# Gated linear attention: the read-out matmuls issued head by head instead of chunk by chunk

## The chip, the cores and the metric

The kernel runs on one core of a Trainium2 chip. The metric is the device time of one execution in microseconds (us); lower is better. The profile is that of one execution, recorded by the hardware profiler; its times are counted from the first instruction.

## The reference

The program computes two model blocks, each with two layers, on 512 tokens of 1024 channels (and, in the first block, 256 context tokens). The change lies in the second block, in its gated linear attention (GLA) with 4 heads, key width 64, value width 128 and chunks of 64 tokens. Each layer runs it twice: forward over time and backward over time. Per direction:

```
b = cumsum(log decay) within a chunk;  ref = b in the middle of the chunk
q_in = q * exp(b - ref);  k_in = k * exp(ref - b)
A = where(mask, q_in @ k_in^T, 0)          # 64x64 per chunk and head
o_intra = A @ v                            # inside the chunk
state_n = state_(n-1) * decay + k_state^T @ v      # 64x128 per head, chunk after chunk
o_inter = (q * exp(b)) @ state             # what earlier chunks contribute
o = o_intra + o_inter                      # forward and backward are summed, then RMS-normalised
```

## The kernel before

All activations lie channel-major in SBUF, 128 channels by up to 512 tokens. The large products split each fp32 operand into a high and a low part and run three matmuls (hi*hi, hi*lo, lo*hi); `single`, called through `in_unit(n)`, is one such product of 24 matmuls (lines 841 on). Weights stream from HBM through a ring of four slots: SyncE loads, ScalarE (line 1178) makes the high part, GpSimd (line 464) the low part. Every engine has its own program, written out by hand in order, and they meet at semaphores; nothing is reordered by a scheduler.

In a second-block layer TensorE interleaves the input products `in_unit(2)` to `in_unit(18)` with the pieces of the GLA. These are, for a direction d (0 forward, 1 backward):

- `turned_keys(d)` (line 902): 8 transposes of 128x128; ScalarE copies them.
- `updates(d, p)` (line 918): for a pair of heads, 16 matmuls of 64 rows by 64 columns that make k^T v of each chunk; VectorE runs the recurrence over chunks (lines 2448 and 2450).
- `a_tiles(d, t0)` (line 932): the scores of two 128-token tiles, 4 heads each; contraction over the 64 key channels, so each matmul uses 64 of the array's 128 rows. Heads 0 and 2 (e = 0) take rows 0 to 63, heads 1 and 3 (e = 1) rows 64 to 127. VectorE masks them (`masked`, line 2461).
- `o_tile(d, t)` (lines 945 and 955), which the change touches: the output of a 128-token tile. It waits once, for the masked scores; nothing inside it waits. Line 945 is `A @ v`: 4 matmuls, one for each head, that contract over 128 tokens and use all 128 rows, 128 columns of output. Line 955 is `q @ state`: for each of the tile's two 64-token chunks and each head one matmul that contracts over 64 key channels (64 rows, again halves by e = head % 2) and writes 64 columns. Head h accumulates in its own PSUM bank (bank 4 + h). One chunk of each direction has no earlier state and so no such matmul: chunk 0 forward (in tile 0), chunk 7 backward (in tile 3).

All of these operands are fp32. The hardware runs such a matmul as two passes, and the trace records each pass: 4 matmuls are 8 records, 8 matmuls 16.

The order on TensorE around it is: `a_tiles(0,0)`, `in_unit(8)`, `o_tile(0,0)`, `o_tile(0,1)`, `a_tiles(0,2)`, `in_unit(9)`, `o_tile(0,2)`, `o_tile(0,3)`, `turned_keys(1)`, `in_unit(10)`, five matmuls of a sum of squares (line 1011), `updates(1,0)`; and in the backward direction the same from `a_tiles(1,0)`, ending with `in_unit(16)` after `o_tile(1,3)`. VectorE's own order has, beside the GLA's element-wise work, `unit_out(n)` (line 2386), which empties the product of `in_unit(n)` out of PSUM, and, in the first of the two layers alone, the rotation tables (lines 2336 to 2354), which stand between `unit_out(9)` and `unit_out(10)`. The fourth of the five matmuls of line 1011 writes the PSUM bank that `unit_out(10)` empties.

Of the kernel before, what the change touches and what calls it, by code (L numbers as in the profile page):

```python
# [24 lines left out]
P = 128  # L25
# [23 lines left out]
GLA_HEADS, GLA_PAIRS, GLA_C = 4, 2, 64  # L49
# [81 lines left out]
def two_blocks(nc, weights, ada_w, pool_w, vec1_d, vec2_d, gla_w_d, x_d, cond_d, ple_d, pos_d, consts_d, rope_d,  # L131
# [4 lines left out]
    with ctx:  # L136
# [42 lines left out]
        PS = ctx.enter_context(nc.psum_tensor("ps", [P, SLOTS * 1024], f32))  # L179
        ADA_PS = 3 * 1024 + 512  # L180

        def ps(s, a=0, b=None):
            return PS[:, s * 1024 + a:s * 1024 + b]
# [14 lines left out]
        def ada_sums(p, q=slice(0, P)):  # L198
# [26 lines left out]
        GF, GQI, GKI, GQX, GKS, GKT, GST, GAM = (M0, M0 + 1024, M0 + 2048, M0 + 3072, M0 + 4096, M0 + 5120,  # L225
                                                 M0 + 6144, M0 + 8192)
# [76 lines left out]
        def on(l, name):  # L303

            if (l // LAYERS, name) not in named:
                named[l // LAYERS, name] = sem(f"block{l // LAYERS}_{name}")
            return named[l // LAYERS, name]

        def at_least(l, name, n):

            return on(l, name), n + per_layer[name] if l % LAYERS else n
# [19 lines left out]
        def halves(a):  # L331

            return a.rearrange("p (a b) -> p a b", a=2)
# [9 lines left out]
        def latent(buf, n):  # L343

            if n < 2:
                return buf[:, :].rearrange("p (c t) -> p c t", c=CH)[:, 4 + 2 * n:6 + 2 * n, SEQ:TOK]
            return halves(buf[:, n * TOK:n * TOK + SEQ])
# [5 lines left out]
        def slot_of(l, st, n):  # L353

            return (UNIT0[l, st] + n) % SLOTS

        def taken(l, st, t, k):

            return k + USE[l, st][t] + 1
# [115 lines left out]
        def _(pe):  # L475
# [361 lines left out]
            def block2(l):  # L837
# [38 lines left out]
                def gv(rows, t, h):  # L876
                    c = (2 * t + h // 2) * TOK + SEQ + (h % 2) * P
                    return X[rows, c:c + P]

                every = slice(0, P)  # L880
# [56 lines left out]
                def o_tile(d, t):  # L937
                    first = 0 if d == 0 else GLA_CHUNKS - 1
                    pe.wait_ge(*at_least(l, "a_read", d * 4 + t + 1))
                    if d == 0 and t == 0:  # L940
                        for s in (2, 3):
                            pe.wait_ge(tile_free[s], taken(l, "gla_o", s, 0))
                    for h in range(GLA_HEADS):
                        o0 = 2048 + h * 512
                        nc.tensor.matmul(PS[:, o0 + t * P:o0 + (t + 1) * P], gv(every, t, h),
                                         AR[:, GAM + (t % 2) * 512 + h * P:GAM + (t % 2) * 512 + (h + 1) * P],
                                         start=(d == 0 and t == 0), stop=False, skip_group_check=True)
                    todo = [n for n in (2 * t, 2 * t + 1) if n != first]
                    for n in todo:
                        for h in range(GLA_HEADS):  # L950
                            p, e = h // 2, h % 2
                            o0 = 2048 + h * 512
                            q0 = GQX + p * SEQ + n * GLA_C
                            s0 = GST + (p * GLA_CHUNKS + n) * P
                            last = nc.tensor.matmul(PS[:, o0 + n * GLA_C:o0 + (n + 1) * GLA_C],
                                                    AR[64 * e:64 * e + 64, s0:s0 + P], AR[64 * e:64 * e + 64, q0:q0 + GLA_C],
                                                    start=False, stop=(d == 1 and t == 3 and n == todo[-1]),
                                                    skip_group_check=True)
                    last.then_inc(on(l, "o_mm"), 1)
# [18 lines left out]
                for u in range(SLOTS):  # L978
                    s = slot_of(l, "gv", u)
                    pe.wait_ge(units_split, nth_done(l, "gv", u))  # L980
                    for n, (w, act) in enumerate(((WH, XH), (WH, XL), (WL, XH))):
                        for k in range(2):
                            for t in range(4):
                                c = 2 * u + k
                                last = nc.tensor.matmul(PS[:, 2048 + t * SEQ:2048 + (t + 1) * SEQ], act[:, c * TOK + t * P:c * TOK + (t + 1) * P],  # L985
                                                        w[:, s * UNIT + k * 512:s * UNIT + (k + 1) * 512],
                                                        start=(c == 0 and n == 0), stop=(c == CH - 1 and n == 2))
# [8 lines left out]
                a_tiles(0, 0)  # L996
                in_unit(8)
                o_tile(0, 0)
                o_tile(0, 1)
                a_tiles(0, 2)  # L1000
                in_unit(9)
                o_tile(0, 2)
                o_tile(0, 3)
                turned_keys(1)
                in_unit(10)
                for n in range(Q_CH + KV_CH):
                    s, first, end, k_use = (1, 0, Q_CH, 3) if n < Q_CH else (0, Q_CH, Q_CH + KV_CH, 4)
                    if n == first:
# [3 lines left out]
                                     start=n == first, stop=n == end - 1).then_inc(on(l, "rmsq_used"), 1)  # L1012
# [28 lines left out]
                for at_, j in enumerate(UQ_ITEMS):  # L1041
                    t = at_ % 2
                    pe.wait_ge(tile_free[t], taken(l, "uq", t, at_ // 2))
                    if j in ("rope0", "rope1", "rope2"):
                        n = int(j[-1])
# [9 lines left out]
                    for n, (w, act) in enumerate(((WH, XH), (WL, XH), (WH, XL))):  # L1055
                        for k in range(nk):
# [6 lines left out]
                            if j < 10:  # L1063
                                last = nc.tensor.matmul(halves(ps(t, 0, SEQ)), w[:, ws * UNIT + (o + k) * P:ws * UNIT + (o + k + 1) * P],  # L1064
                                                        latent(act, k0 + k), start=(n == 0 and k == 0),
                                                        stop=(n == 2 and k == nk - 1))
                            else:
                                q = j - 10
                                last = nc.tensor.matmul(ps(t, 0, SEQ), act[:, a0 + q * P:a0 + (q + 1) * P],
                                                        w[:, ws * UNIT + k * 512:ws * UNIT + (k + 1) * 512],  # L1070
                                                        start=(n == 0 and k == 0), stop=(n == 2 and k == nk - 1))
# [41 lines left out]
                n = 4 * MLA_HEADS  # L1113
# [19 lines left out]
                for c in range(CH):  # L1133
                    s, u, t = c % 4, slot_of(l, "pp", c // 4), c % 2
# [3 lines left out]
                    for n, (w, act) in enumerate(((WH, XH), (WH, XL), (WL, XH))):  # L1138
                        for k in range(2):
                            last = nc.tensor.matmul(  # L1140
                                ps(t, 0, SEQ).rearrange("p (a b) -> p a b", a=2), w[:, u * UNIT + (s * 2 + k) * P:u * UNIT + (s * 2 + k + 1) * P],
                                act[:, :].rearrange("p (c t) -> p c t", c=CH)[:, 2 * k:2 * k + 2, SEQ:TOK],
                                start=(n == 0 and k == 0), stop=(n == 2 and k == 1))
# [1651 lines left out]
```

## Time and profile before

| | us |
|---|---|
| median of 3 runs | 3294.37 |
| lowest and highest | 3292.84, 3294.6 |
| the profiled execution | 3294.6 |
| its span, first to last instruction | 3292.8 |
| TensorE busy in it | 3153.2 (96%) |
| VectorE busy | 1961.4 (60%) |
| ScalarE busy | 1138.0 (35%) |
| GpSimd busy | 849.9 (26%) |

The profiled execution is 0.2 us above the median and 1.8 us above its own span, so a difference of spans may be read as a difference of times. The second block's two layers take roughly the last 750 us; their GLA stretches are about 2600 to 2700 us and 2970 to 3065 us.

### The profile page before, as it was taken

The page shows a single profiled execution, that of the slowest core. Times are in us where ns is not written, and L with a number is a line of the kernel's source. Part 1 is how long each engine was busy: PE and PEld are TensorE (multiplying, and loading weights), DVE is VectorE, ACT ScalarE, POOL GpSimd, SP SyncE. Part 2 cuts the span into 40 slices and gives each one's busy share as a digit, 9 for nine tenths or more (in the row PEclk, how much of TensorE's full clock was granted, in tenths as well). Part 3 has the DMA queues.
Part 4 walks back from the last instruction along what each step waited for, and adds up shares of the span by engine and source line. Part 5 has one row for each costly group of instructions (what it writes and reads, how often), then busy time and mean ns, then how long its engine had stood idle before and what let it go on. Part 6 is the DMA issues. An engine that isn't in the chain of part 4 may idle for free.

```text
span 3292.8 us, 43512 instructions
## 1 busy us (share of the span) xinstructions
PE 3153.2 (96%) x16010; PEld 2481.9 (75%) x16010; DVE 1961.4 (60%) x2687; ACT 1138.0 (35%) x1615; POOL 849.9 (26%) x336
## 2 busy tenths in 40 slices
PE   6999999999989999998999999999999999999998
PEld 4778877788878888886777677768886775777765
DVE  4787887663566254356878875674646655255433
ACT  2212254234232221124333535343224435343533
POOL 1001200233323222231012034434443321332312
PEclk8999999999999999999999999999999999999999
DMA  7452100112112111224531022322323211222211
GB/s 273 154 179 77 39 14 27 45 58 96 64 45 64 58 64 64 64 65 147 188 125 45 1 77 83 125 77 91 101 91 98 77 59 45 66 84 68 84 39 64
DMA packets 75307, 270.50 MB, mean 82 GB/s; under 512 B 8592, under 2 KB 9616, under 8 KB 74512
## 3 DMA queue, kind: packets, MB, share of 16 engines
q1 hardware_dynamic: 71376, 256.04, 23.3%
q10 hardware_dynamic: 3776, 12.32, 1.0%
q8 instruction: 107, 1.75, 0.2%
q14 instruction: 48, 0.39, 0.0%
HBM read 263.87 MB, written 4.46 MB: 81 GB/s over the span
## 4 chain that ended last, share of the span: by engine, by line
PE 84%; DVE 9%; DVEq 2%; ACT 2%; issue 1%; DMA 1%; SPq 0%; ACTq 0%
PE ps L537 49%; PE ps L842 11%; PE ps L503 4%; PE ps L653 2%; PE ps L776 2%; PE ps L985 1%; DVE arena L2063 1%; PE ps L674 1%; PE ps L641 1%; PE ps L798 1%; DVE x L2071 1%; PE ps L1064 1%; PE ps L756 1%; PE ps L1084 1%; PE ps L586 1%
## 5 line engine op out<-in xcount | busy, mean ns | idle before, releaser
L464 POOL TENSOR_TENSOR w_lo<-w_raw,w_hi 128x1024 fp32r<-128x1024 f32 x332 | 849.7, 2562 | 2406.9 <-ACT w_hi L1178 2406.9
L1178 ACT ACTIVATE w_hi<-w_raw 128x1024 fp32r<-128x1024 f32 x380 | 399.2, 1054 | 553.1 <-PE ps L537 296.7
L537 PE MATMUL ps<-act_hi,w_hi 128*128 128x512 f32 (+1 forms) x2608 | 552.3, 361 | 7.6 <-ACT arena L1412 1.8
L537 PE MATMUL ps<-act_lo,w_hi 128*128 128x512 f32 (+1 forms) x2608 | 535.8, 354 | 0.0
L537 PE MATMUL ps<-act_hi,w_lo 128*128 128x512 f32 (+1 forms) x2608 | 535.4, 354 | 0.0
L537 PEld LDWEIGHTS ps<-act_hi,w_hi 128*128 128x128 f32 x2608 | 427.7, 188 | 126.3 <-issue 50.4
L537 PEld LDWEIGHTS ps<-act_hi,w_lo 128*128 128x128 f32 x2608 | 428.4, 188 | 72.4
L537 PEld LDWEIGHTS ps<-act_lo,w_hi 128*128 128x128 f32 x2608 | 428.1, 188 | 72.3 <-issue 0.5
L1911 DVE SCALAR_TENSOR_TENSOR x<-ps,mod,x 128x512 f32<-128x512 f32 x96 | 60.2, 659 | 295.2 <-PE ps L537 238.4
L2071 DVE SCALAR_TENSOR_TENSOR x<-arena,vec,x 128x512 f32<-128x512 f32 x336 | 230.4, 713 | 0.0
L2063 DVE SCALAR_TENSOR_TENSOR arena<-arena,vec 128x783 f32<-128x783 f32 (+1 forms) x240 | 227.8, 949 | 0.2 <-issue 0.2
L2294 DVE SCALAR_TENSOR_TENSOR arena<-arena,vec 128x769 f32<-128x769 f32 (+1 forms) x88 | 160.4, 1823 | 16.0 <-issue 16.0
L1244 ACT ACTIVATE arena<-ps,vec 128x768 f32<-128x768 f32 (+3 forms) x64 | 50.8, 794 | 281.2 <-PE ps L537 194.8
L842 PE MATMUL ps<-act_hi,w_hi 128*128 128x512 f32 x432 | 117.8, 406 | 8.9 <-ACT act_hi L1524 6.2
L1832 DVE TENSOR_TENSOR ffn_lo<-arena,ffn_hi 128x768 f32 (+1 forms) x44 | 119.0, 2704 | 6.5
L842 PE MATMUL ps<-act_hi,w_lo 128*128 128x512 f32 x432 | 111.7, 392 | 0.0
L842 PE MATMUL ps<-act_lo,w_hi 128*128 128x512 f32 x432 | 111.5, 391 | 0.0
L776 PE MATMUL ps<-arena 128*128 128x256 f32 (+1 forms) x288 | 103.7, 480 | 6.0 <-ACT tmp L1283 6.0
L2291 DVE TENSOR_SCALAR arena<-arena,vec 128x769 f32<-128x769 f32 (+1 forms) x44 | 29.1, 661 | 132.5 <-ACT arena L1496 132.5
L1496 ACT ACTIVATE arena<-ps 128x512 f32<-128x512 f32 x66 | 32.4, 526 | 213.9 <-PE ps L537 211.1
L842 PEld LDWEIGHTS ps<-act_hi,w_hi 128*128 128x128 f32 x432 | 79.3, 189 | 35.5 <-issue 18.4
L653 PE MATMUL ps<-arena 128*128 128x256 f32 x416 | 103.1, 381 | 1.6 <-ACT arena L1400 1.5
(336 smaller groups left out, 4411.8 us busy)
## 6 DMA issues: line engine op xcount, KB each, us to landing
w_raw<-in_weights SPq DMA_DIRECT2D x380, 512.0 KB, 3.5
arena<-in_ada_w SPq DMA_DIRECT2D x75, 512.0 KB, 4.6
tmp<-in_ada_w SPq DMA_DIRECT2D x21, 512.0 KB, 4.3
x<-in_x SPq DMA_DIRECT2D x2, 1536.0 KB, 20.0
x<-in_x ACTq DMA_DIRECT2D x1, 3072.0 KB, 10.7
arena<-in_pool_w ACTq DMA_DIRECT2D x2, 1024.0 KB, 4.8
x_mid<-x ACTq DMA_DIRECT2D x1, 2048.0 KB, 7.4
x<-x_mid ACTq DMA_DIRECT2D x1, 2048.0 KB, 8.6
```

Source lines behind the costliest of these rows:

```text
L464: nc.gpsimd.tensor_tensor(WL[:, w], raw, WH[:, w].bitcast(f32), ALU.subtract).then_inc(units_split, 1)
L503: last = nc.tensor.matmul(ps(tb + s, a, b), w[:, s * UNIT + k * P:s * UNIT + (k + 1) * P], act[:, k * TOK + a:k * TOK + b], start=(n == 0 ...
L537: last = nc.tensor.matmul(ps(t, a, b), w[:, s * UNIT + k * P:s * UNIT + (k + 1) * P], act[:, k * TOK + a:k * TOK + b], start=(n == 0 and k ...
L653: last = nc.tensor.matmul(ps(3, (m % 2) * 512, (m % 2) * 512 + 2 * P), values(m, k), AR[:, a:a + 2 * P], start=(k == 0), stop=(k == nk - 1))
L776: last = nc.tensor.matmul(ps(it % 2, a, b), AR[:, q:q + P], AR[:, k + a:k + b], start=True, stop=True)
L842: return nc.tensor.matmul(out, w0[:, k0:k0 + P], act[:, k * n:k * n + SEQ], start=start, stop=stop)
L1178: nc.scalar.activation(WH[:, s * UNIT:(s + 1) * UNIT], RAW[:, (s % 2) * UNIT:(s % 2 + 1) * UNIT], ACT.Copy).then_inc(hi_done, 1)
L1832: return V.tensor_tensor(lo, src, hi.bitcast(f32), ALU.subtract)
L1911: last = V.scalar_tensor_tensor(x, ps(t, a, b), at(MOD, mod(l, gate, j, m), 1), x, ALU.mult, ALU.add)
L2063: t = V.scalar_tensor_tensor(acc, src, w, acc, ALU.mult, ALU.add)
L2071: t = V.scalar_tensor_tensor(acc, src, w, acc, ALU.mult, ALU.add)
L2294: t = V.scalar_tensor_tensor(cv, src, w, cv, ALU.mult, ALU.add)
```

## The change

The loop over heads becomes the outer one: each head issues its full-row matmul and right behind it its half-row matmuls of both chunks. The same matmuls run on the same data into the same banks with the same waits; only their order changes, and the first matmul of each bank still clears it.

```diff
@@ o_tile(d, t)
                     for h in range(GLA_HEADS):
+                        p, e = h // 2, h % 2
                         o0 = 2048 + h * 512
-                        nc.tensor.matmul(PS[:, o0 + t * P:o0 + (t + 1) * P], gv(every, t, h),
-                                         AR[:, GAM + (t % 2) * 512 + h * P:GAM + (t % 2) * 512 + (h + 1) * P],
-                                         start=(d == 0 and t == 0), stop=False, skip_group_check=True)
-                    todo = [n for n in (2 * t, 2 * t + 1) if n != first]
-                    for n in todo:
-                        for h in range(GLA_HEADS):
-                            p, e = h // 2, h % 2
-                            o0 = 2048 + h * 512
+                        todo = [n for n in (2 * t, 2 * t + 1) if n != first]
+                        last = nc.tensor.matmul(PS[:, o0 + t * P:o0 + (t + 1) * P], gv(every, t, h),
+                                                AR[:, GAM + (t % 2) * 512 + h * P:GAM + (t % 2) * 512 + (h + 1) * P],
+                                                start=(d == 0 and t == 0), stop=False, skip_group_check=True)
+                        for n in todo:
                             q0 = GQX + p * SEQ + n * GLA_C
                             s0 = GST + (p * GLA_CHUNKS + n) * P
                             last = nc.tensor.matmul(PS[:, o0 + n * GLA_C:o0 + (n + 1) * GLA_C],
...
```

TensorE's program in the first direction of the first such layer, `o_tile(0,0)` and `o_tile(0,1)` between a product (L842) and the next scores (L932), before. L945 is the full-row matmul, L955 the half-row one:

```order
 L842 MATMUL ps<-act_lo,w_hi 128x512 x8
-L945 MATMUL ps<-arena,x 128x128 x4
-L955 MATMUL ps<-arena 128x64 x4
-L945 MATMUL ps<-arena,x 128x128 x4
-L955 MATMUL ps<-arena 128x64 x8
```

There are two runs of full-row and two of half-row matmuls. The same place in the changed program, where the two lines are L947 (full rows) and L953 (half rows); of the second tile the first head stands here, and the three others repeat it:

```order
+L947 MATMUL ps<-arena,x 128x128
+L953 MATMUL ps<-arena 128x64
+L947 MATMUL ps<-arena,x 128x128
+L953 MATMUL ps<-arena 128x64
+L947 MATMUL ps<-arena,x 128x128
+L953 MATMUL ps<-arena 128x64
+L947 MATMUL ps<-arena,x 128x128
+L953 MATMUL ps<-arena 128x64
+L947 MATMUL ps<-arena,x 128x128
+L953 MATMUL ps<-arena 128x64 x2
```

Every full-row matmul now stands alone between half-row ones, and the one or two half-row matmuls behind it are of one head, so of one half of the rows. On the other engines no instruction moves.

## Rows read from the trace of the kernel before

**Rows 1.** The page: busy time of each engine, and the chain of waits by engine.
```profile
PE 3153.2 (96%) x16010; PEld 2481.9 (75%) x16010; DVE 1961.4 (60%) x2687; ACT 1138.0 (35%) x1615; POOL 849.9 (26%) x336
...
PE 84%; DVE 9%; DVEq 2%; ACT 2%; issue 1%; DMA 1%; SPq 0%; ACTq 0%
```
**Rows 2.** Lines 945, 955 and 1011 (first layer): count, shortest/median/longest ns, first and last start.
```profile
L945 PE MATMUL ps<-arena,x x128: 270/275/377, 2626.0 to 3064.2; 128*128 128x128 f32 x128
...
L955 PE MATMUL ps<-arena x224: 272/272/320, 2627.0 to 3064.8; 64*128 64x64 f32 x112
...
L1011 PE MATMUL ps<-arena,ones x10: 590/593/1223, 2646.8 to 2657.4; 128*128 128x512 f32 x10
```
**Rows 3.** TensorE's timeline, forward direction: start, duration (us), instructions, [idle before].
```profile
2625.99 1.05 PE L945 MATMUL ps<-arena,x 128*128 128x128 f32 x8
...
2627.57 1.16 PE L945 MATMUL ps<-arena,x 128*128 128x128 f32 x8
2628.65 1.11 PE L955 MATMUL ps<-arena 64*128 64x64 f32 x16
2629.60 1.11 PE L932 MATMUL ps<-arena 64*128 64x128 f32 x16
...
2636.21 1.05 PE L945 MATMUL ps<-arena,x 128*128 128x128 f32 x8
...
2638.23 1.16 PE L945 MATMUL ps<-arena,x 128*128 128x128 f32 x8
...
2640.36 1.09 PE L902 MATMUL ps<-ident,arena 128*128 128x128 f32 x8
```
**Rows 4.** The same timeline to 2687.02 us, cut inside the second tile.
```profile
2686.59 0.28 PE L955 MATMUL ps<-arena 64*128 64x64 f32 x2
2686.80 0.49 PE L945 MATMUL ps<-arena,x 128*128 128x128 f32 x2
```
**Rows 5.** The same, cut at 2685.93 us, inside the first tile's half-row run.
```profile
2685.56 0.28 PE L945 MATMUL ps<-arena,x 128*128 128x128 f32 x1
2685.76 0.44 PE L955 MATMUL ps<-arena 64*128 64x64 f32 x4
```
**Rows 6.** The same timeline in the later attention, half rows of one head only.
```profile
2755.33 1.12 PE L1084 MATMUL ps<-arena 64*128 64x512 f32 x2
2756.39 0.66 PE L1094 MATMUL ps<-ident,tmp 128*128 128x128 f32 x4
```
**Rows 7.** The same timeline from the end of the forward direction on.
```profile
2646.76 2.74 PE L1011 MATMUL ps<-arena,ones 128*128 128x512 f32 x6
2654.65 3.78 PE L1011 MATMUL ps<-arena,ones 128*128 128x512 f32 x4 [5.15 <-DVE arena L2386]
2658.36 1.99 PE L918 MATMUL ps<-x,arena 64*64 64x128 f32 x32
2660.28 2.10 PE L842 MATMUL ps<-act_hi,w_hi 128*128 128x512 f32 x8
...
2665.93 1.10 PE L918 MATMUL ps<-x,arena 64*64 64x128 f32 x32
```
**Rows 8.** TensorE's waits, 2560 to 2730 us and 2935 to 3090 us: total, times, longest.
```profile
PE ps L1011 <- DVE arena L2386: 5.2, 1, 5.2
PE ps L842 <- ACT vec L1213: 0.4, 1, 0.4
```
**Rows 9.** VectorE's timeline, first layer, forward direction.
```profile
2632.18 1.44 DVE L2461 COPY_PREDICATED arena<-gla_masks,ps 128x256 f32<-128x256 int32 x4
...
2653.90 0.69 DVE L2386 TENSOR_TENSOR arena<-ps,vec 128x512 f32<-128x512 f32 x1 [0.19 <-issue]
```
**Rows 10.** Stretches: busy us (count) of PE, PEld, DVE, ACT, POOL; granted clock; DMA.
```profile
2654.60:2660.20 5.60, 5.55 (x36) 2.77 (x36) 0.00 (x0) 1.65 (x3) 0.00 (x0) 0.50 0.02 3
2684.70:2699.20 14.50, 14.50 (x131) 12.70 (x129) 8.13 (x11) 4.22 (x5) 7.46 (x4) 1.00 0.49 146
```
**Rows 11.** ScalarE's timeline, first layer, behind the forward direction.
```profile
2651.11 0.67 ACT L1211 ACTIVATE vec<-ps,cst 128x512 f32<-128x512 f32 x1
```

## The prediction

> **What bounds the kernel now.** I read the page first: TensorE is busy 96% of the span and holds 84% of the chain of waits [rows 1]. So TensorE time anywhere is end time, unless a wait near it absorbs it. Next comes the count of what the change touches: 128 records of line 945 and 224 of line 955 [rows 2], which is 64 full-row and 112 half-row matmuls, two records each, in 16 tiles (2 layers, 2 directions, 4 tiles). All 16 follow one of four patterns, so one direction read closely is enough: TensorE's timeline of it [rows 3], then cut finely for the gaps between single records [rows 4, 5]. Last come TensorE's waits around the GLA [rows 8]: one of 5.2 us in the first layer, 0.4 us in the second. Where there is no wait, the loss or gain of a tile counts in full; at the one wait I must follow VectorE as well.
>
> **What a tile costs now.** Starts of groups give the four tiles of a direction [rows 3]: 2625.99 to 2627.57 is 1.58 us (tile 0, one chunk), then 2.03, 2.02 (2636.21 to 2638.23) and 2.13 (to 2640.36): 7.76 us. In more detail, with the start of one record to the start of the next:
> - full to full, steady: eight records take 1.05 and one lasts 0.275 [rows 2, 3], so (1.05 - 0.275)/7 = 0.11.
> - full to half, the rows switched: last L945 at 2685.56, first L955 at 2685.76 [rows 5]: 0.20, so 0.09 beyond the pace.
> - the first two pairs of half records: four records end at 0.44, each lasts 0.272 [rows 2, 5]: 0.16 apart. Steady: sixteen take 1.11, the last pair begins at 0.84, (0.84 - 0.16)/6 = 0.11 for each pair. Two records at a time, one on each half of the rows.
> - half to full: last pair at 2686.59, L945 at 2686.80 [rows 4]: 0.205 by the middle of the roundings. The first two full records then take 0.49 with one lasting 0.275: 0.215 apart instead of 0.11.
>
> So a change between full and half rows costs about 0.14 one way (0.09 + 0.05) and 0.19 the other (0.09 + 0.10): the array is emptied and the next weights cannot be loaded early. The Trainium skill says the same in "TensorEngine Tiling (Array Packing)", Key Properties: changing the tiling mode drains the engine. It gives no figure; the rows have it.
>
> **What a tile costs afterwards.** The pairs vanish, since consecutive half matmuls belong to one head and so to one half of the rows, and the switches rise from 2 in a tile to 8. A head of a two-chunk tile is: full to full 0.215, full to half 0.20, half to half 0.16, 0.11, 0.11, half to full 0.205: 1.00 us. A head of a one-chunk tile: 0.215 + 0.20 + 0.16 + 0.205 = 0.78. That half records of one half of the rows keep 0.11 follows from the pairs: each half of the rows takes its next record after 0.11. That the switch costs as much with only one half in use is seen in the later attention [rows 6]: two half records of 512 columns take 2755.33 to 2756.39 = 1.06, and such a record passes at (2.74 - 0.59)/5 = 0.43 [rows 2, 7]; 1.06 - 0.86 = 0.20 for drain and uncovered load.
> Tile 0, after a full-row product: 4 x 0.78 - 0.10 = 3.02. Tile 1, with no switch behind it (L932 is half-row): 4 x 1.00 - 0.10 = 3.92. Tile 2: 3.91. Tile 3: 4.02. Together 14.87, against 7.76: **+7.11 us for a direction**. The backward direction has the one-chunk tile last; it is put together from the same gaps before and after, so its increase is the same.
>
> **What hides it.** In the second layer nothing: TensorE waits 0.4 us in 155 [rows 8], and VectorE and ScalarE follow it. Both directions count: +14.2. In the first layer the backward direction has no wait behind it either: +7.1. The forward direction of the first layer runs into the 5.15 us wait before the fourth of the five matmuls of line 1011 [rows 7]. It waits for VectorE's L2386 at 2653.90, which stands at the end of an unbroken run of VectorE work [rows 9]. VectorE itself is delayed only where it needs something late: the masks at 2632.18 need the scores of L932, which end at 2629.60 + 1.11 = 2630.71 and leave it 1.47 us of margin. The two tiles ahead of them cost (3.02 - 1.58) + (3.92 - 2.03) = 3.33 more, so VectorE slips by 1.86. TensorE arrives 7.11 later, VectorE releases it 1.9 later, and 7.11 - 5.15 = 1.96: they arrive together, and the wait is replaced by no wait, at +1.96.
>
> Then something is given back. Behind the 5.15 us of idleness the granted clock is 0.50, which is 1.2 GHz, from 2654.60 to 2660.20 [rows 10]. There line 1011 takes 3.71 us (2654.65 to 2658.36) for four records where 4 x 0.43 = 1.72 would do at the full 2.4 GHz, and line 918 takes 1.99 where its twin at 2665.93 takes 1.10 [rows 7]. That is 1.99 + 0.89 = 2.88 us. With the idleness gone I expect the clock to stay, so this direction ends at 1.96 - 2.88, or -0.9. What could be late next is the bank that ScalarE's L1211 must read before the next product: it ended at 2651.11 + 0.67, 5.0 behind the end of the product at 2646.76 [rows 7, 11]; 7.1 later that is 2658.9, and the product that needs it would start at 2660.28 - 0.9 = 2659.4. Covered by half a microsecond.
>
> **The sum.** 3 x 7.11 = 21.3, less 0.9: +20.4. On the profiled execution's own 3294.6 us this is **3315.0 us**; the median of the runs shown is 0.2 lower, which changes nothing.
>
> **The rivals.**
> - *The clock does not come back in the first layer, or a later idle spot meets it differently:* the 2.9 us stay, 3317.9 us. For it: the idle may not vanish wholly. 10%.
> - *The loads over a switch are fetched ahead, and only the drain of 0.09 remains.* A head is then four gaps of 0.11 and two of 0.20, 0.85 with the roundings, or 0.63 with one chunk, and a direction 2.52 + 3.33 + 2 x 3.42 = 12.7, +4.9. Three of them, and in the first layer 0.8 less 2.9: +12.6, 3307.2 us. Against it: the 0.21 and 0.16 of [rows 4, 5]. 9%.
> - *The loads of one half of the rows do not hide behind its own matmuls,* so every half to half gap is 0.16. This adds 0.096 for each two-chunk head, 12 heads in a direction, 1.15 for each of four directions (TensorE is the late one in the first layer too): 3319.6 us. Against it: full-row records start 0.11 apart on the same rows although each has a load of its own, and pairs keep 0.11. 6%. The Trainium skill has this as a rule ("TensorE: Matmul & The Clock Gate", Part 3, The mechanism: loads overlap running matmuls only where the row group differs). By it the sum would be this rival's; the rows speak against it.
> - *The clock falls inside the new stretches,* because the array works less in them. Two tiles are up to 8 us in which the records leave the array empty at every switch. The one fall in these rows costs 2.9 us; one for each of the eight stretches is +23: 3338 us. Against it: the trace shows full clock over tiles with two switches each [rows 10], and in none of these rows does it fall while TensorE has work. 5%.
> - *A switch costs nothing when only one or two records lie between, and only the pairing is lost:* 16 and 24 slots of 0.112, 9.9 us for a direction, +2.1 each; the forward one of the first layer stays in its wait. +6.3, 3300.9 us. 4%.
> - *Not slower.* If besides that a half record of 64 columns passed in half the time of a 128-column one (0.056) on its own half of the rows, the pairing would have been worth nothing and the switches saved would decide: tiles of 1.34 and 1.79, 6.7 us for a direction, -1.05 each, 3291.4 us. It needs both a free switch and a load faster than 0.11; the turning point is a head of 0.5 us instead of 1.0. Every row of the pairs shows 0.11. 2%.
> - *Nothing is absorbed in the first layer*, since VectorE slips as far as TensorE: 21.3 + 7.1, 3323.0 us. It would need a VectorE instruction that waits for the last tile. 2%.
>
> The forecast itself has the remaining 62%, with a range of its own of 3311.5 to 3318.5: 0.02 us of error in a head's length is 1.3 us over the 64 heads, and the clock or a slower VectorE instruction beside GpSimd may move it by 2. The range for 8 in 10 is 3306 to 3320.5; it takes in the cheaper switch, the lost clock and the uncovered loads. What a measurement of this kernel can tell from no change is about 0.2%, 6.6 us. Slower by more than that: 94%. Within it: the free switch and the not-slower case, 5%. Faster: 1%.
>
> **What would show it.** In the changed profile TensorE's busy records of these lines keep their count and their durations, but the timeline of a tile shows the head's full and half records alternating with about 1.0 us for each head and a tile of 3.9 to 4.0 us. The wait before line 1011 in the first layer should be gone or under 0.5 us, and the granted clock behind it 1.00. The scores' masks on VectorE in that layer should start near 2634. The second layer's GLA should be 14 us longer, with no wait of TensorE to explain it. The forecast is wrong if a head takes 0.85 or less (the load is fetched ahead), if half records of one head stand 0.16 apart throughout, or if the clock is below 1.00 between the tiles.

## The result and the profile after

| | before | after |
|---|---|---|
| median, us | 3294.5 | 3342.4 |
| lowest and highest | 3292.8, 3300.6 | 3340.3, 3344.8 |
| span of the profiled execution | 3292.8 | 3339.0 |

The changed kernel is slower: 1.014 times before, with a 95% interval of 1.0128 to 1.0152. The forecast was 3315.0 with a range up to 3320.5, so the direction was right and the size was less than half of what came: +20 forecast, +48 measured.

The page of the changed kernel, first the span, then the busy time of each engine, then the chain of waits by engine:

```profile
span 3339.0 us, 43512 instructions
...
PE 3207.3 (96%) x16010; PEld 2520.0 (75%) x16010; DVE 1953.8 (59%) x2687; ACT 1138.2 (34%) x1615; POOL 848.3 (25%) x336
...
PE 85%; DVE 8%; DVEq 2%; ACT 2%; issue 1%; DMA 1%; SPq 0%; ACTq 0%
```

The 46.2 us of span are TensorE's: it is busy for 54 us more, while no other engine's busy time moved by more than 8 us [rows 1]. Its timeline in the forward direction of the first layer, the changed kernel's answer to [rows 3] and [rows 7] (start, duration, instructions; L947 full rows, L953 half rows; ps<-act are the matmuls of a product, which leave one record each):

```profile
2625.79 0.38 PE L947 MATMUL ps<-arena,x 128*128 128x128 f32 x2
...
2626.46 0.49 PE L947 MATMUL ps<-arena,x 128*128 128x128 f32 x2
...
2627.24 0.49 PE L947 MATMUL ps<-arena,x 128*128 128x128 f32 x2
...
2629.99 0.80 PE L947 MATMUL ps<-arena,x 128*128 128x128 f32 x2
2630.71 1.11 PE L953 MATMUL ps<-arena 64*128 64x64 f32 x4
2631.76 0.79 PE L947 MATMUL ps<-arena,x 128*128 128x128 f32 x2
...
2637.10 3.35 PE L842 MATMUL ps<-act_hi,w_hi 128*128 128x512 f32 x8
2640.28 2.01 PE L842 MATMUL ps<-act_hi,w_lo 128*128 128x512 f32 x8
...
2643.94 0.38 PE L947 MATMUL ps<-arena,x 128*128 128x128 f32 x2
2644.26 0.66 PE L953 MATMUL ps<-arena 64*128 64x64 f32 x4
2644.84 0.49 PE L947 MATMUL ps<-arena,x 128*128 128x128 f32 x2
2645.26 0.66 PE L953 MATMUL ps<-arena 64*128 64x64 f32 x4
2645.84 0.49 PE L947 MATMUL ps<-arena,x 128*128 128x128 f32 x2
...
2661.36 4.45 PE L1009 MATMUL ps<-arena,ones 128*128 128x512 f32 x10
2665.74 1.10 PE L918 MATMUL ps<-x,arena 64*64 64x128 f32 x32
2667.22 2.06 PE L842 MATMUL ps<-act_hi,w_hi 128*128 128x512 f32 x8 [0.38 <-ACT vec L1211]
```

A two-chunk head takes 1.00 us (2644.84 to 2645.84) and a one-chunk head 0.78 (2626.46 to 2627.24), exactly what the gaps of before gave. But from about 2629.7 on the same two-chunk head takes 1.77 (2629.99 to 2631.76), and the dense product behind it takes 3.35 us for eight matmuls that take 2.01 a little later. The stretches tell why (busy us of PE, PEld, DVE, ACT, POOL, then the granted clock):

```profile
2629.70:2639.80 10.10, 10.10 (x42) 8.30 (x42) 4.81 (x11) 2.19 (x4) 2.35 (x1) 0.50 0.28 101
2650.10:2656.80 6.70, 6.70 (x25) 5.63 (x25) 5.86 (x12) 1.19 (x2) 0.00 (x0) 0.50 0.23 78
2691.70:2697.70 6.00, 6.00 (x38) 4.87 (x36) 0.69 (x1) 2.56 (x3) 3.35 (x2) 1.00 0.51 171
2697.90:2704.50 6.60, 6.60 (x32) 5.52 (x32) 1.62 (x5) 0.00 (x0) 2.34 (x1) 0.50 0.50 159
2715.00:2721.60 6.60, 6.60 (x19) 4.98 (x18) 0.00 (x0) 2.06 (x4) 0.00 (x0) 0.50 0.24 79
```

The granted clock falls to 0.50, 1.2 GHz, while TensorE is busy without a gap, four to six microseconds after the tiles begin. It does so in each of the eight pairs of tiles. In the second layer it shows in the timeline, where two full-row records that take 0.49 us at full clock take 0.79, and four half-row ones 1.11 instead of 0.66:

```profile
3025.83 0.80 PE L947 MATMUL ps<-arena,x 128*128 128x128 f32 x2
...
3042.76 1.11 PE L953 MATMUL ps<-arena 64*128 64x64 f32 x4
...
3091.49 0.79 PE L947 MATMUL ps<-arena,x 128*128 128x128 f32 x2
```

The fourth such place there is at 3108.12 us. Before, the same tiles ran at 1.00, in the pairs of [rows 10] and in those of the three other directions. The changed kernel's 21 executions all have a mean granted clock of 0.979 to 0.981, those of the kernel before 0.986 to 0.989, so the falls are not a matter of the one execution that was profiled.

What a fall costs can be read off. The first pair and its product took 2625.99 to 2636.21 = 10.22 us [rows 3] and take 2625.79 to 2643.94 = 18.15: 7.93 more, of which the tiles at full clock account for 3.33 and the fall, 10.1 us long, for 4.6. The second took 10.55 us (2636.21 to 2646.76, [rows 3, 7]) and takes 17.42: 6.87 more, 3.78 and, for a fall of some 6.7 us, 3.1. In exchange the 13.52 us from there to the product at 2660.28 [rows 7] are now 5.86: the wait of 5.15 us is gone, the sum of squares (line 1009, formerly 1011) and line 918 run at full speed, and a wait of 0.38 us for ScalarE's square root is new. This direction ends at 7.93 + 6.87 - 7.66 = +7.1 us, where -0.9 was forecast. For the three others 21.3 was forecast. Read pair by pair in both timelines they take 39.8 us more, so each of their six falls costs 3.05 to 3.13 us, 18.4 together. The span grew by 46.2 us, 0.7 less than these parts add up to.

### The profile page after: what moved, and what is told of

Its sections match the earlier page's. It is cut to its first block, busy times and chain, and to the rows that moved or that the text cites. A ratio compares the mean times of both kernels' runs of the same rounds, so it can differ in the third digit from the quotient of the medians.

```text
span 3339.0 us, 43512 instructions
## 1 busy us (share of the span) xinstructions
PE 3207.3 (96%) x16010; PEld 2520.0 (75%) x16010; DVE 1953.8 (59%) x2687; ACT 1138.2 (34%) x1615; POOL 848.3 (25%) x336
## 4 chain that ended last, share of the span: by engine, by line
PE 85%; DVE 8%; DVEq 2%; ACT 2%; issue 1%; DMA 1%; SPq 0%; ACTq 0%
PE ps L537 48%; PE ps L842 12%; PE ps L503 4%; PE ps L653 2%; PE ps L776 2%; PE ps L983 1%; DVE arena L2061 1%; PE ps L953 1%; PE ps L674 1%; PE ps L641 1%; PE ps L798 1%; DVE x L2069 1%; PE ps L1062 1%; PE ps L756 1%; PE ps L1082 1%
## 5 line engine op out<-in xcount | busy, mean ns | idle before, releaser
L537 PEld LDWEIGHTS ps<-act_hi,w_hi 128*128 128x128 f32 x2608 | 427.7, 188 | 126.8 <-issue 50.9
L842 PE MATMUL ps<-act_hi,w_hi 128*128 128x512 f32 x432 | 127.5, 432 | 9.2 <-ACT act_hi L1522 6.2
L842 PEld LDWEIGHTS ps<-act_hi,w_hi 128*128 128x128 f32 x432 | 86.3, 206 | 38.6 <-issue 19.8
L842 PE MATMUL ps<-act_hi,w_lo 128*128 128x512 f32 x432 | 112.8, 395 | 0.0
L842 PE MATMUL ps<-act_lo,w_hi 128*128 128x512 f32 x432 | 111.6, 392 | 0.0
```

Of the source, the lines that this page charges most:

```text
L537: last = nc.tensor.matmul(ps(t, a, b), w[:, s * UNIT + k * P:s * UNIT + (k + 1) * P], act[:, k * TOK + a:k * TOK + b], start=(n == 0 and k ...
L842: return nc.tensor.matmul(out, w0[:, k0:k0 + P], act[:, k * n:k * n + SEQ], start=start, stop=stop)
```

## The experiments

Theory A: the 27 us that the forecast missed are these falls (24 in the first expectation, which sets the span of 3339.0 against the time of 3315.0), and the clock falls because a long run of bare heads leaves the array too little to do. Theory B: the switches bring it down by themselves. Theory C: the lost pairing does, since half of the rows stand idle. Each time below is a median beside the kernel before on the same chip, which stood at 3292.8 to 3293.3 us there; a ratio has its 95% interval behind it. Expectations that start from 3294.5 are therefore 1.5 us too high throughout, and what counts is the difference. The diffs are shortened: `full` is the full-row matmul of a head, `half_rows` the half-row one of a head and chunk, and where a lone `+` block stands it is the new order of a tile with two chunks.

**Dense work between the heads.** All switches and all unpaired matmuls stay; only the next product's matmuls are moved.

```diff
+for h in range(GLA_HEADS):          # in o_tile, behind the head's matmuls
+    for step in steps[:2]: step()   # two of the 24 matmuls of in_unit(9), (10), (15) or (16)
+    del steps[:2]
```

What is left of the product follows where the whole of it stood.

> The changed order, but behind each head of a tile stand two of the 24 full-row, 512-column matmuls of the next input product, which otherwise follow the two tiles in one run. The work and the number of switches between full and half rows are those of the changed kernel (the product's matmuls take the place of the next head behind a half run); 8 switches in a tile, half matmuls unpaired. Theory A (the 24 us that the forecast missed are falls of the granted clock, and it falls because in a stretch of bare heads the array has too little work): with 0.45 us of dense work behind each head of 1.00 us the clock stays at full in and behind the tiles, and the time is the forecast's 3315 us, perhaps 2 to 4 more because the masks of the second pair of tiles now have a third of a product to hide behind. Theory B (the switches themselves bring the clock down, whatever stands between them): the clock falls as in the changed kernel and the time stays near 3342 us.

3316.0 us, 1.0069 of before (1.0052 to 1.0085). The timeline of this kernel in the first layer (L939 full, L948 half rows), and the granted clock over both pairs:

```profile
2645.10 0.38 PE L939 MATMUL ps<-arena,x 128*128 128x128 f32 x2
2645.42 0.66 PE L948 MATMUL ps<-arena 64*128 64x64 f32 x4
2646.00 0.73 PE L842 MATMUL ps<-act_hi,w_lo 128*128 128x512 f32 x2
2646.57 0.38 PE L939 MATMUL ps<-arena,x 128*128 128x128 f32 x2
```

```profile
2625.30:2636.20 10.90, 10.90 (x57) 8.43 (x55) 5.98 (x6) 2.26 (x5) 4.55 (x2) 1.00 0.14 48
2639.20:2651.00 11.80, 11.80 (x66) 9.51 (x66) 10.78 (x18) 1.58 (x2) 2.50 (x1) 1.00 0.14 46
```

A head with two product matmuls takes 1.47 us (2645.10 to 2646.57), the head's 1.00 and 0.45 of product, so every switch is paid as before. The clock stays at 1.00, here and in the other six stretches, and of the changed kernel's loss of 48 us 23 are left, 25 gone. That is what theory A expects, and it puts the kernel near the forecast's 3315 us (+20.4 forecast, +23.0 measured, 17 to 28): the sum of the forecast holds where the clock is full. Theory B in its plain form has fallen.

**One matmul instead of two.**

```diff
-    for step in steps[:2]: step()
+    for step in steps[:1]: step()      # and del steps[:1]
```

> As the run with two matmuls of the next input product behind each head, but with one: half the dense work (0.23 us) behind a head of 1.00 us. Theory A (the clock falls where bare heads follow each other because the array is too little filled): in between, so either the clock stays in all eight stretches and the time is 3316 us as with two, or it falls in some of them for each 3 us more. Under the rival, that any dense work at all between heads hides the fall, the same 3316; so this run tells how much is needed and not whether. 3340 would mean that one is as good as none.

3314.5 us, 1.0063 (1.0046 to 1.0079). The same as with two: 0.23 us of dense work behind each head is already enough in all eight stretches.

**Pairing lost, switches kept at two.**

```diff
-for n in todo:
-    for h in range(GLA_HEADS):      # halves of the rows alternate
+for h in (0, 2, 1, 3):              # heads of rows 0-63 first, then of rows 64-127
+    for n in todo:
```

> Only the pairing is lost: a tile issues its four full-row matmuls, then the half-row ones of heads 0 and 2 and then those of heads 1 and 3, so that neighbours share one half of the rows; 2 switches in a tile as before the change. At full clock a two-chunk tile grows by 8 slots of 0.112 less one overlap at the border, 0.85 us, a one-chunk tile by 0.4, a direction by 2.95; three directions count, the first layer's forward one stays inside its wait: 3294.5 + 8.9 = 3303 us. Theory A: a tile of 2.9 us has 0.9 us of dense full-row work in it, so the clock may stay, 3303 us. Theory C (half matmuls on one half of the rows bring the clock down): it falls in each of the eight stretches, 3 us each, 3327 us.

3298.3 us, 1.0012 (1.0003 to 1.0022). No fall in any tile, so theory C in its plain form has fallen too, and it costs less than expected, +5.3 us (1.0 to 7.2) against +8.9. In the timeline of this kernel the half-row run takes 1.53 us (2636.68 to 2638.21), where the 16 records took 2637.19 to 2638.23, 1.04, before; 0.49 more instead of 0.85. First the row of before, then this run's; the last excerpt is the border to the scores of L932:

```profile
2637.19 1.11 PE L955 MATMUL ps<-arena 64*128 64x64 f32 x16
```

```profile
2636.68 1.60 PE L948 MATMUL ps<-arena 64*128 64x64 f32 x16
2638.21 1.16 PE L939 MATMUL ps<-arena,x 128*128 128x128 f32 x8
```

```profile
2628.65 0.37 PE L932 MATMUL ps<-arena 64*128 64x128 f32 x1
2628.75 0.27 PE L948 MATMUL ps<-arena 64*128 64x64 f32 x1
2628.86 0.27 PE L932 MATMUL ps<-arena 64*128 64x128 f32 x1
```

L932 stands behind all of L948 in the program and begins before it is through: by the program's order these are matmuls for the free half of the rows that start ahead of earlier ones for the busy half. Inside the run it is the same. Its sixteen records stand in two rows of eight, each 0.11 us apart behind a first gap of 0.16: one starts from 2636.68 to 2637.51, the other from 2637.18 to 2638.01. So where an unpaired run changes the half, part of the pairing comes back.

**Switches added, pairing kept: six in a tile.**

```diff
+full(0); full(1)
+for i, n in enumerate(todo):
+    half_rows(0, n); half_rows(1, n)      # a pair: rows 0-63 and 64-127
+    full(2 + i)
+for n in todo: half_rows(2, n); half_rows(3, n)
```

> Only switches are added: half matmuls stay in pairs of both halves of the rows, but the full-row matmuls of heads 2 and 3 stand between them, 6 switches in a two-chunk tile and 4 in a one-chunk one where there were 2 before. Each added pair of switches costs 0.34 at full clock: 0.68 and 0.34 in a tile, 2.4 in a direction, three of them: 3294.5 + 7.1 = 3302 us. If the drains alone bring the clock down (theory B), 3 us more in each of up to eight stretches, 3326 us. If it is lost pairing (theory C), or thin work (theory A, a tile of 2.7 us is still mostly filled), it stays at 3302.

3299.0 us, 1.0017 (1.0008 to 1.0027): +6.1 us where +7.1 was expected, which this comparison can't tell apart. No tile has a fall of the clock. The two-chunk tile costs what was worked out: the excerpt's first and last row are the starts of two tiles, 2.70 us apart, against 2.02 [rows 3].

```profile
2633.60 0.60 PE L939 MATMUL ps<-arena,x 128*128 128x128 f32 x4
...
2636.30 0.71 PE L939 MATMUL ps<-arena,x 128*128 128x128 f32 x4
...
2650.80 1.98 PE L1025 MATMUL ps<-arena,ones 128*128 128x512 f32 x4 [2.56 <-DVE arena L2400]
```

The last row has something that the expectation left out, though the forecast had it: the wait before the fourth matmul of the sum of squares is only 2.56 us now, and behind it four records take 1.98 us instead of 3.78 [rows 7]. The clock did not fall there, and in this execution, at 3295.5 us one of the two fastest of its ten, the 2.9 us of that fall came back.

**Eight switches in a tile, pairing kept.**

```diff
+for f, hs in ((0, (0, 1)), (1, (0, 1)), (2, (2, 3)), (3, (2, 3))):
+    full(f)
+    for h in hs: half_rows(h, todo[f % 2])     # chunks 0, 1, 0, 1
```

> As many switches as in the changed kernel, 8 in a two-chunk tile, but behind each full-row matmul stand two half-row ones of two heads that use both halves of the rows at once (one-chunk tiles: 4 and 8). A group is 0.215 + 0.20 + 0.16 + 0.205 = 0.78 us, a tile 3.1, a direction 3.5 more than before; three of them: 3293 + 10.5 = 3303.5 us at full clock. The switches come more often than in the changed kernel (every 0.39 us against every 0.50). Theory B (drains bring the clock down): it falls in most stretches, 20 us more. Theory C (lost pairing, half of the rows idle): it stays. [...]

3301.6 us, 1.0023 (1.0013 to 1.0032): +8.8 us against the expected +10.5. The timeline of two groups, and the clock over the second pair of tiles:

```profile
2641.96 0.49 PE L939 MATMUL ps<-arena,x 128*128 128x128 f32 x2
2642.38 0.44 PE L948 MATMUL ps<-arena 64*128 64x64 f32 x4
2642.75 0.49 PE L939 MATMUL ps<-arena,x 128*128 128x128 f32 x2
```

```profile
2639.70:2645.90 6.20, 6.20 (x50) 4.68 (x48) 5.72 (x9) 1.58 (x2) 2.51 (x1) 1.00 0.26 85
```

A group takes 0.79 us, so the switches come more often than in the changed kernel, and the clock stays at 1.00 in all eight stretches. So neither the number of switches nor their rate is enough by itself. In these runs the clock fell only where both came together, switches and half matmuls that leave the other half of the rows idle. That need not be a rule about the two: the same matmuls of a two-chunk tile take 2.0 us before, 2.5 unpaired, 2.7 with six switches, 3.1 with eight and 4.0 in the changed order, and it fell in the slowest alone. The runs do not separate the combination from mere thinness, which is theory A in its plain form.

**The changed order in every second tile.**

```diff
+if t % 2:   # the changed order
+else:       # the order of before
```

> The changed order in the second tile of each pair only; the first keeps the old one. Bare heads stand for 4 us instead of 8. At full clock: +3.3 in the first layer's backward direction, +7.1 in the second layer, +0.4 in the forward one of the first layer (masks 0.4 late), 3304 us, or 3301 if the idle spot there shrinks enough to keep the clock. Theory A with a stretch of 8 us needed: 3301 to 3304. If four microseconds of bare heads are enough to bring the clock down, 3 us more in each stretch, up to 3327.

3311.5 us, 1.0058 (1.0041 to 1.0074): between the two expectations. The granted clock of this kernel in the first layer, inside the bare heads of tile 1, inside those of tile 3, and behind these:

```profile
2625.00:2629.00 4.00, 4.00 (x37) 3.43 (x36) 3.75 (x6) 0.59 (x2) 0.00 (x0) 1.00 0.40 131
2636.80:2640.20 3.40, 3.40 (x22) 2.74 (x20) 3.17 (x4) 0.77 (x1) 2.45 (x1) 1.00 0.00 0
2640.40:2647.00 6.60, 6.60 (x22) 5.60 (x23) 5.76 (x12) 1.19 (x2) 0.00 (x0) 0.50 0.22 79
```

One tile of bare heads, 3 to 4 us, can bring the clock down, and in this profile did so in four of eight stretches, two of them in the first layer; one of the four falls was half as long as the others (3.4 us). Which ones depends on something that the instructions do not show: the forward tile 3 fell in the first layer and not in the second, the forward tile 1 in the second and not in the first.

**The first layer's forward direction alone.**

```diff
+if l == LAYERS and d == 0:   # the changed order
+else:                        # the order of before
```

> The changed order only in the forward direction of the first layer, the one that ran into the wait of 5.15 us. The forecast had it at -0.9 us in all, with the clock at full level throughout: 3292 us. Theory A with the trace of the changed kernel, in which the clock fell twice there and the same work ended 7.1 us later than before: 3293 + 7 = 3300 us. If the falls were the doing of the later stretches alone, 3292.

3301.4 us, 1.0024 (1.0014 to 1.0034). The mean granted clock over most of each pair and the start of what follows it:

```profile
2627.00:2640.00 13.00, 13.00 (x57) 10.64 (x57) 7.72 (x14) 2.20 (x4) 2.41 (x2) 0.61 0.23 82
2645.00:2655.00 10.00, 10.00 (x47) 8.47 (x48) 8.94 (x14) 1.72 (x3) 2.50 (x1) 0.72 0.16 52
```

The clock falls in both, and behind them the wait of 5.15 us is gone, as in the changed kernel. So the -0.9 us of the forecast is +8.1 here (4.6 to 11.2) and +7.1 in the changed kernel's timeline, and the falls need nothing of the later stretches.

**Two tiles together.** Fewer switches than before.

```diff
+for tt in (t, t + 1): full(tt, h) for all h
+for tt in (t, t + 1): half_rows(tt, h, n) for all n, h
```

> Fewer switches than the kernel before: two tiles are done together, eight full-row matmuls and then all their half-row ones in pairs. Two switches of 0.14 + 0.19 us vanish in each pair of tiles: 0.34 us, six pairs count (the two of the first layer's forward direction lie before its wait): 3294.5 - 2.0 = 3292.5 us. If a switch costs only a drain of 0.09 it is 3293.4. The clock is not expected to fall anywhere that it does not before the change. Not to be told from no change if the waits of the masks, needed 0.5 us earlier now, take it back.

3291.7 us, 0.9995 (0.9985 to 1.0004): not to be told from no change. The timeline has the gain, 2633.11 to 2636.92 = 3.81 us for a pair that took 2636.21 to 2640.36 = 4.15 [rows 3], but six times 0.34 is less than this comparison resolves (3 us either way).

```profile
2633.11 1.95 PE L939 MATMUL ps<-arena,x 128*128 128x128 f32 x16
2634.99 2.00 PE L948 MATMUL ps<-arena 64*128 64x64 f32 x32
2636.92 1.09 PE L902 MATMUL ps<-ident,arena 128*128 128x128 f32 x8
```

**The idle spot removed.** The order of before; one instruction of VectorE is moved forward.

```diff
 for dst, quarter in ((SIN2, 0.0), (COS2, 0.25)):    # rotation tables
+    if dst == COS2: unit_out(10)
...
-unit_out(10)                                         # behind the tables, first layer only
```

> The order of the kernel before, and on VectorE in the first layer unit_out(10) between the halves of the rotation tables: the wait of 5.15 us before the fourth matmul of the sum of squares goes, and with it the fall of the clock behind it. By the rows of before 5.15 + 2.88 = 8.0 us, less 0.4 us that ScalarE's square root then makes the next product wait: 3293 - 7.6 = 3285 us. If the clock falls for another reason than the idleness, the 2.9 us stay and it is 3288. With two tiles together it was 3283.2, so this run also says whether the fewer switches are worth their 2 us.

3286.3 us, 0.9978 (0.9968 to 0.9989). TensorE's timeline of this kernel:

```profile
2643.51 4.45 PE L1018 MATMUL ps<-arena,ones 128*128 128x512 f32 x10
2647.89 1.10 PE L918 MATMUL ps<-x,arena 64*64 64x128 f32 x32
2649.37 2.08 PE L842 MATMUL ps<-act_hi,w_hi 128*128 128x512 f32 x8 [0.38 <-ACT vec L1220]
```

From the sum of squares to the product it takes 5.86 us instead of 13.52 [rows 7]; 5.15 are the wait and 2.9 the clock, less the 0.38 of the new wait. That part of the forecast's reading was sound. In the median the gain is 7.0 us (3.6 to 10.5) where 7.6 was expected.

**Both together.** The diffs of the last two runs in one kernel.

> A version meant to beat both kernels: two tiles together (as in the run of that name), and on VectorE in the first layer unit_out(10) is put between the two halves of the rotation tables instead of behind them, so that the fourth matmul of the sum of squares finds its bank empty. The wait of 5.15 us there goes, and with it the fall of the clock behind it, 2.9 us. Together with the 2 us of fewer switches: 3293 - 10 = 3283 us, provided that VectorE, which then still has half of the tables ahead of the recurrence over chunks, does not become late for the second half of the updates (it would begin 1 to 3 us after it could). If that wait takes the place of the old one, 3286 to 3289; if the 2.9 us are not given back, 3286.

3283.2 us, 0.9971 (0.996 to 0.9983). It beats both kernels, by 9.6 and by some 59 us. Whether the fewer switches add anything to the idle spot's 7.0 us is not shown: the two intervals overlap.

## Why the prediction was wrong

- *Which patterns, how many, what a gap costs:* right. Heads of 1.00 and 0.78 us stand in the timeline, and with dense work between them the whole kernel is 23.0 us slower than before against the 20.4 of the forecast.
- *Half matmuls on one half of the rows keep 0.11; the loads do not hide over a switch:* right; the rivals about it (3307 and 3320 us) would have made a head 0.85 or 1.10 us long.
- *The wait of 5.15 us disappears and gives back the clock behind it:* right in kind and size, 7.7 us with the 0.38 us wait that is new. With dense work between the heads, where no fall delays TensorE, the ten records of the sum of squares stand together too (4.45 us from 2653.69). The half microsecond of cover that the prediction saw was not there because it followed the wrong instruction: the product waits for the second half of ScalarE's inverse square root, L1211 now and L1213 before, and not for the first half, the L1211 of before [rows 11]. The same wait of 0.4 us stood in the second layer already [rows 8]. In the changed kernel the masks began at 2637.21, behind a wait of VectorE of 5.14 us for L932, and not near 2634: the fall had slowed the scores too.

```profile
2637.21 1.44 DVE L2459 COPY_PREDICATED arena<-gla_masks,ps 128x256 f32<-128x256 int32 x4 [5.14 <-PE ps L932]
```

- *The clock stays up, since TensorE is never idle:* this is the step that failed. The sum had the clock at 1.00 in all eight new stretches and so nothing for it there; it fell to 0.50 in each, for 26 us in all. The prediction took idleness as the only cause because each fall that it looked at had an idle spot ahead of it, and it read tiles with two switches at full clock as evidence for tiles with eight. The rival that it gave 5%, one fall of about 2.9 us in each of the eight stretches and 3338 us, is what happened: eight falls, about 3.1 us each and 4.6 for the first. The places and the price were written down, but the chance was far too low and the range left it out. Its reason, that the array works less there, fits every run and is not singled out by them.

The sum, then, over the span's 46.2 us: four directions of 7.11 us, 28.4; less 7.7 at the idle spot; and 26.1 for the eight falls, 7.7 in the first layer's forward direction and 18.4 in the six other stretches, all read from the timelines. That is 46.9; the 0.7 us over were not traced. The run with dense work checks it from the other side: without the falls 25 us are gone.

What stays open is which property of a stretch decides. Six or eight switches in a tile with the pairing kept did not bring the clock down, nor did unpaired matmuls with two switches, and with 0.23 us of dense work behind each head it stayed. The runs do not tell a need for both from work that is merely spread too thin, and nothing in them tells the four falling stretches of the run with every second tile from the four others.

## What to carry to other kernels

Group matmuls by how many rows of the array they use, and within a half-row group let the halves alternate; the order of issue alone was worth 48 us here. When a change thins out TensorE's work without idling it, read the granted clock as something that can change and price it as half speed over the rest of the stretch and the dense work behind it, here about 3 us a fall. If a thin stretch can't be avoided, put matmuls of the next product between its pieces rather than behind them.

## What the runs showed of the hardware

- The granted clock fell to 0.50 with TensorE busy without a gap, in runs of matmuls that switched between full and half rows every 0.4 to 0.6 us with one half of the rows idle during the half-row ones (eight of eight stretches of 7 to 8 us, four of eight of 3 to 4 us); one 512-column matmul behind each head kept it at 1.00.
- A switch costs about 0.14 us from full to half rows and 0.19 back, whether one half of the rows is used behind it (0.42 us for the full-row and 0.58 for the half-row part of a changed two-chunk head) or both (0.42 and 0.37 in a group of the run with eight switches and the pairing kept).
- Half-row matmuls for a free half of the rows begin before earlier ones for the busy half (2628.65 against 2628.75 us in the run with unpaired matmuls), which made an unpaired run cost 0.49 us in place of 0.85.
- Before the fourth matmul of the sum of squares, a wait of 2.56 us (six switches) left the clock at full, where one of 3.62 us (unpaired matmuls) and those of 5.15 us (before) and 5.66 us (two tiles together) had it at 0.50 behind them.
